# A narrower pad in SBUF: the weight buffers move from byte 64 to byte 32 of each 128, the inner feed-forward inputs from 0 to 96

## What is computed

```python
mod = silu(c) @ w_ada + b_ada                    # six rows of 2048
h = modulate(rmsnorm(x, g_norm_mix), shift_m, scale_m)
proj = h @ w_in                                  # then attention
x = x + gate_m * (attention(proj) @ w_out)
h = modulate(rmsnorm(x, g_norm_ffn), shift_f, scale_f)
f = square(relu(h @ w_ff1)) @ w_ff2              # 2048 -> 8192 -> 2048
x = x + gate_f * f
```

## The kernel before

| buffers | before | after |
|---|---|---|
| `xT`, `acts` | 0 | 0 |
| `raw`, `hi`, `lo`, `ada_ring`, `cross`, `consts` | 64 | 32 |
| `mods`, `silu`, `tables`, `wi`, `top8` | 64 | 32 |
| `vecs` | 96 | 64 |
| `cols`, `small` | 0 | 96 |
| `work`, `proj`, `y`, `f_acts` | 0 | 96 |

## Time and profile before

### The profile page before, as it was taken

How to read it: one execution, slowest core, us unless ns; L and a number is a source line. 1 busy time by engine, 2 the same in 40 slices (tenths; PEclk the granted TensorE clock), 3 DMA queues, 4 the chain that set the end, 5 groups by cost and what they waited for, 6 DMA issues and landing times.

```text
span 2920.0 us, 54982 instructions
## 1 busy us (share of the span) xinstructions
PE 2737.8 (94%) x21794; PEld 2576.0 (88%) x21794; DVE 1926.7 (66%) x2008; ACT 1119.8 (38%) x1261; POOL 172.2 (6%) x281
## 2 busy tenths in 40 slices
PE   5799999899999999989999959989889999999998
PEld 1486778899999999989899749989889999999998
DVE  1446587787777867766767765778657556565655
ACT  2224443343344433333343343433334444343433
POOL 5000000101001000100000000000100000000000
PEclk8799999899999999989999979999979999999998
DMA  9887766579888877756756604548646666575653
GB/s 369 333 295 262 244 195 227 173 273 305 283 292 280 297 263 246 264 183 195 252 180 205 223 0 144 188 165 286 237 132 209 215 212 229 193 243 201 218 198 111
DMA packets 299828, 658.62 MB, mean 226 GB/s; under 512 B 30688, under 2 KB 37176, under 8 KB 295224
## 3 DMA queue, kind: packets, MB, share of 16 engines
q1 hardware_dynamic: 267448, 539.41, 54.1%
q0 software_dynamic: 32256, 117.45, 12.4%
HBM read 654.69 MB, written 2.10 MB: 225 GB/s over the span
## 4 chain that ended last, share of the span: by engine, by line
PE 84%; DVE 6%; DMA 5%; ACT 2%; issue 2%; SPq 0%; DVEq 0%; ACTq 0%; POOLq 0%
PE ps L1601 24%; PE ps L1603 23%; PE ps L1602 23%; DMA proj<-in_w_ada 2%; PE ps L1646 2%; PE ps L1648 1%; PE ps L1647 1%; DVE lo L890 1%; PE ps L1699 1%; PE ps L2006 1%; ACT hi L543 1%; DMA ada_ring<-in_w_ada 1%; PE ps L1764 1%; DMA raw<-in_w_ff 1%; PE ps L1689 1%
## 5 line engine op out<-in xcount | busy, mean ns | idle before, releaser
L890 DVE TENSOR_TENSOR lo<-raw,hi 128x1024 fp32r<-128x1024 f32 x868 | 1050.1, 1222 | 710.4 <-ACT hi L543 708.3
L543 ACT ACTIVATE hi<-raw 128x1024 fp32r<-128x1024 f32 x868 | 911.1, 1059 | 1358.6 <-PE ps L1603 1073.7
L1601 PE MATMUL ps<-acts,hi 128*128 128x256 f32 x4432 | 1253.4, 283 | 43.6 <-DVE acts L1330 19.7
L1602 PE MATMUL ps<-acts,hi 128*128 128x256 f32 x4432 | 1239.4, 280 | 0.0
L1603 PE MATMUL ps<-acts,lo 128*128 128x256 f32 x4432 | 1238.8, 280 | 0.0
L1601 PEld LDWEIGHTS ps<-acts,hi 128*128 128x128 f32 x4432 | 843.2, 190 | 75.7 <-issue 57.5
L1602 PEld LDWEIGHTS ps<-acts,hi 128*128 128x128 f32 x4432 | 842.4, 190 | 3.6 <-issue 3.1
L1603 PEld LDWEIGHTS ps<-acts,lo 128*128 128x128 f32 x4432 | 844.7, 191 | 0.3
L1601 PE MATMUL ps<-f_acts,hi 128*128 128x256 f32 x2048 | 568.4, 278 | 5.6 <-DVE lo L890 5.6
L1602 PE MATMUL ps<-f_acts,hi 128*128 128x256 f32 x2048 | 567.6, 277 | 0.0
L1603 PE MATMUL ps<-f_acts,lo 128*128 128x256 f32 x2048 | 567.6, 277 | 0.0
(11 more groups left out here) (237 smaller groups left out, 1508.2 us busy)
## 6 DMA issues: line engine op xcount, KB each, us to landing
raw<-in_w_ff SPq DMA_DIRECT2D x512, 512.0 KB, 4.6
raw<-in_w_in SPq DMA_DIRECT2D x232, 512.0 KB, 4.6
ada_ring<-in_w_ada POOLq DMA_DIRECT2D x224, 512.0 KB, 4.9
proj<-in_w_ada SPq DMA_DIRECT2D x32, 1024.0 KB, 8.5
ada_ring<-in_w_ada SPq DMA_DIRECT2D x44, 512.0 KB, 4.5
work<-in_w_ada SPq DMA_DIRECT2D x32, 512.0 KB, 4.4
raw<-in_w_out SPq DMA_DIRECT2D x32, 512.0 KB, 5.0
raw<-in_w_o SPq DMA_DIRECT2D x32, 512.0 KB, 4.9
```

The costliest lines, as they stand in the source:

```text
L543: nc.scalar.activation(hi[n % SPLIT][:, :], raw[n % RAW][:, :], ACT.Copy).then_inc(hi_ready, 1)
L890: V.tensor_tensor(lo[n % SPLIT][:, :], raw[n % RAW][:, :], hi[n % SPLIT][:, :].bitcast(F32), ALU.subtract)\
L1601: M(out, h, right[:, 0:S], start=start, stop=False)
L1602: M(out, h, right[:, S:2 * S], start=False, stop=False)
```

## The change

The unused buffer between `acts` and the rings is 8 float32 wide in each partition in place of 16. No instruction, wait, transfer or order is changed; every buffer behind it begins 32 bytes lower.

```diff
         xT = sb("xT", [P, KT, S])
         acts = sb("acts", [P, KT, 2 * S], F32R)
-        sb("weights_shift", [P, 16])
+        sb("weights_shift", [P, 8])
         raw = [sb(f"raw{i}", [P, CHUNK]) for i in range(RAW)]
         hi = [sb(f"hi{i}", [P, CHUNK], F32R) for i in range(SPLIT)]
         lo = [sb(f"lo{i}", [P, CHUNK], F32R) for i in range(SPLIT)]
```

## The result

The kernel with the 32-byte pad took 2972.4 us (median of 4 runs, 2969.3 to 2977.9) beside 2937.6 us of the kernel before in the same session (4 runs, 2915.3 to 2940.2): a ratio of 1.0137, with a 95% interval of 1.0086 to 1.0189. It is slower by 1.4%. The forecast, 2935 us and no measurable change, was wrong; the time lies inside the stated range, near the 2982 of the slower rival. The mean granted clock of the profiled executions was 0.955 beside 0.953 before, so the loss is not one of clock.

A forecast was written before the change was run, and what follows sets the result against it. The prediction took TensorE, through the pace of its matmuls, to bound the kernel. Its terms summed to +1 us on 2921.7, giving 2923 for the profiled execution; it put the median at 2935 us, range 2908 to 2984.

The forecast's parts named there:

- slower rival: `acts` products lose the clean distance of 64 and are held up: +25 to +46 us, 2982 us; chance 0.32.
- What bounds the kernel, and that only the pace can change it: TensorE, busy 94%, bounds the kernel; what counts is how fast the 19,440 matmuls of `product` follow each other.
- `acts` products, 0 us taken: 13,296 matmuls whose distance between weights and stream goes from 64 to 32: 0 us, bounds -11 to +46 us.
- The price from `ki2`, 2.3 ns at distance 0: Second tiles in phase `ki2`, read as distance 0, cost 2.3 ns per matmul; on fast `acts` products +25 us.
- `f_acts` products, 0 us because the distance is kept: 6,144 matmuls with weights at 32 and stream at 96, still 64 apart: 0 us if distance is what matters.
- Value groups, VectorE, ScalarE, transfers: Value groups 0 us; VectorE and ScalarE passes 0, between -1 and +2; transfers +1 us, between 0 and +5.
- The spread of the kernel before as a draw of the two paces: Runs 22.5 us apart with the same instructions probably hold different amounts of the slower pace, drawn anew at each TensorE stop.
- The faster rival: At distance 32 TensorE's slow pace doesn't occur, or less after a stop: at least -13 us, 2908 us; chance 0.11.
- The third rival: The fast pace of the matmuls itself loses its 6.6 ns surplus: -128 us, 2809 us; chance 0.03.
- The Trainium skill's rule: TensorE reads weights and stream through independent ports, so buffer places can't matter and the change is exactly 0.

The follow-up runs named there:

- e2: Kernel before with every buffer 96 bytes later, all distances between weights and streams kept: 2939.1 us, ratio 0.9991.
- e5: Kernel before with buffer `small` moved right behind the pad, putting both weights at 192 by 256 in place of 64: 2984.5 us, ratio 1.0177.
- e7: Kernel before with `small` behind the pad and `wi` between `hi` and `lo`: high weights at 192 by 256, low at 64; 2975.2 us, ratio 1.0166.
- The map: Bursts without the kernel's work, both weights at 0 to 240 by 256 in steps of 16, streams at 0: 113.3 ns in all 12 at 64.
- the bursts: Separate kernels running only bursts of 72 products, no other engine at work, with starts of weights and streams varied: 113.3 ns at best.
- e1: Kernel before without any pad, so `acts` products at distance 0 and `f_acts` products still at 64: 2984.6 us, ratio 1.0148.
- e4: Kernel before with only the weights `hi` and `lo` moved to 32 by 128, other buffers on multiples of 64 as before: 3001.7 us, ratio 1.0213.
- e6: Kernel before with `wi` between `hi` and `lo` and `small` behind `lo`: high weights at 64 by 256, low at 192; 2908.9 us, ratio 0.9911.

## Why the prediction was wrong

- **What bounds the kernel, and that only the pace can change it:** right. Busy time of TensorE carries the whole loss, by its pace, and two paces within one kernel were there as described; no unbroken run of over 96 products at a granted clock of 1.00 in the traces of before, e2, e5 and e7 changes from one pace to the other once its first 24 are past. Three readings were off and carried nothing: `product` has 19,440 of 21,794 matmuls, nine tenths and not four fifths; a window counts two or three matmuls too many and not one, so 620 in 70 us is 113.3 ns as elsewhere, not 112.9; and 1446 in 170 us is 117.8.
- **`acts` products, 0 us taken:** this is the step that failed. Measured +3.91 ns each, +50 us, a little over the +46 that stood as the upper bound. The reason given for 0 was that the streams pass over all distances as they run. It doesn't help: where they begin decides. Of the two places known, I called 64 clean and 0 unclean and took 32, as lying between, for harmless, but a middle between two measured points holds only if the effect is smooth. The map shows one narrow good place, and a weak one at 192: 48 and 80 are no better than 32.
- **The price from `ki2`, 2.3 ns at distance 0:** too small by more than half, and it was no price of distance 0. Its second tiles begin at 64 + 576 = 640, so by 256 they lie at 128, where the bursts have 118.6 ns, 5.3 over 113.3; distance 0 costs 119.93 - 113.3 = 6.6 ns (e1). In `ki2` the distance alternates every six matmuls, so probably none of its runs is long enough to settle. After the change the same 60 matmuls take 7.01 us in place of 6.87. By their start times a set of six takes 684 ns in first tiles and 690 ns in second ones before, and 700 ns in both after, at distances of 32 and 96: so the second tiles no longer take more than the first, and both take more than before.
- **`f_acts` products, 0 us because the distance is kept:** right. They were at 113.3 or 117.8 ns as before, and e4 shows what they would have lost without it: another 29 us between the medians.
- **Value groups, VectorE, ScalarE, transfers:** right as far as it matters; passes are unchanged to 0.2% and landings to 0.1 us. The value groups' matmuls add 2 us (the busy time of L1646 to L1648 on the page: 78.3 + 75.8 + 75.8 after, 77.8 + 74.9 + 75.5 before).
- **The spread of the kernel before as a draw of the two paces:** right, by e2 and e6.
- **The rivals:** the slower one, with distance as its condition, is what happened, at a price of 47.6 us between the profiled executions and 35 us between the medians. My argument against it, that the slow pace occurs at distance 64 too, confused two things: a distance of 64 doesn't make the fast pace certain, but at 32 the fast pace never came. The faster rival failed in the change. Its idea, a place where the slow pace doesn't occur, came true in e6 with another arrangement, at 2908.9 us where 2908 had been worked out; that the two agree so closely is luck, since the 2908 took all the surplus of a run at 2937 for slow pace, and the profiled executions of before and e6 lie only 6.2 us apart in span. The third rival didn't occur: 113.3 ns stayed the fastest pace.
- **The Trainium skill's rule** (TensorE: Matmul & The Clock Gate, Part 2, step by step), that loading weights takes nothing from the stream beside it, isn't borne out for these float32r products: by it the place can't matter, but in the bursts no other engine works, and the starts alone move the pace from 113.3 to 120.0 ns. Whether it is bandwidth that the two take from each other, no run shows.

What stays open: why 64 by 256, what happens at a stop that decides between 113.3 and 117.8 ns, and why low weights at 192 beside high weights at 64 had the fast pace in every burst. No run tells either which load meets which stream, since the loads overlap the matmuls (PEld is busy for 2628.9 us beside PE's 2790.7 on the page of after).

## What to carry to other kernels

Where TensorE is the bound and loads weights for every matmul, the byte at which the weights begin against the stream is a term of the time; measure it with bursts at each distance, by 256 and not only by 128, and for each pair of load and stream. A kernel that spreads over more than 1% at the same clock with the same instructions may be drawing its pace: count starts in stretches without a gap, because mean durations hide it. Don't interpolate between two measured places: a point between a good and a bad one has no price until it is measured.

## What the runs showed of the hardware that was not expected

- A matmul of 128 float32r weight columns and 256 stream columns follows the last one after 113.3 ns at best, where 256 columns at the granted 2.4 GHz are 106.7. Of over 50 arrangements of starts none came under it.
- Paces at other starts are 116.7 to 120.1 ns, in a few bursts 122 to 125. The difference between the best and the worst arrangement tried in the whole kernel (e6 to e4, whose kernels of before had 2935.0 and 2936.4 us) is 93 us, 3.2%.
- Shifting everything by 96 bytes changed nothing (0.9991); shifting the weights and what lies behind them up to `cols` by 128 bytes, against both streams, cost 1.8%.
